# Attention stage of a hybrid retention / sparse-attention block: the spread of the transposed row maxima over four heads moved from VectorE to ScalarE

## The chip, the cores and the metric

The kernel runs on one core of one Trainium2 chip. The metric is the device time of one execution in microseconds (us). Every time below is from such executions, or from one profiled execution of the kernel before.

## The reference

One decoder block over 512 tokens of width 1024: RMSNorm and modulation, one joint input projection, retention (4 heads) beside sparse attention (8 query heads in 2 groups, with compressed, selected and window branches), one output projection, a SwiGLU feed-forward layer (width 2816) and a last RMSNorm. The change lies in the softmax of the selected and the window branch:

```python
s_sel = jnp.einsum('bghqd,bgqnld->bghqnl', qi, k_sel).astype(jnp.float32) * scale
...
p_sel = jax.nn.softmax(s_sel, axis=-1)
o_sel = jnp.einsum('bghqnl,bgqnle->bghqe', p_sel, v_sel)
...
s_win = jnp.einsum('bghqd,bgkd->bghqk', qi, k_win).astype(jnp.float32) * scale
p_win = jax.nn.softmax(jnp.where(m_win, s_win, NEG), axis=-1)
```

A sequence of 512 tokens has 8 blocks of 64, and 16 may be selected, so every causal block is selected. Both branches are therefore plain causal softmaxes over 512 keys, with keys and values of their own.

## The kernel before

The program is written by hand for five in-order engines: TensorE (PE), VectorE (DVE), ScalarE (ACT), GpSimd (POOL) and SyncE (SP). Each has its own function, and they meet only at semaphores. Weights are split into a rounded high part and a low rest, so that each product is three matmuls (`product`). The stages are the input projection (units v = 0 to 23, with attention work mixed into the last ones), an attention loop of slots n = 0 to 41, the output projection, the feed-forward layer and the end.

The attention loop works on eight *blocks* x: x = 2i + b is query tile i (128 queries) in branch b (selected, window). Block x has i + 1 *steps*, one for each key tile; `STEP0` gives the first step of each block. Step s has its scores on PE in slot 2s and its `values` product in slot 2s + 3. Scores are computed transposed (keys on partitions, 4 heads x 128 queries on columns), with their sign turned, so the row maximum to be taken off is a minimum here. It must lie along the columns, the same on all partitions. It is made like this:

- PE `pair(x, h)` (line 1317) computes the scores of head h in the other orientation into banks 4 and 5. DVE `row_min` (line 916) takes the minimum over keys into a column of `mcol`. Head h of group g has column 64g + h.
- PE `max_transpose(x)` (line 1323) turns `mcol` into bank 4 (`ps[:, 4, 0:P]`): row 64g + h now holds the minima of head h. It increments `mx_T`.
- `max_rows(x)` (line 920, on DVE) spreads this over four heads: `MB[:, x % 2, h, :]` is the transposed tile times a column of constants that is -1 in the rows with index h modulo 64 and 0 elsewhere (`K_SEL`). It is one operation, 128x128 in PSUM read four times, 128x512 out. It increments `mb_ok`.
- PE line 1350, the last product of `scores`, multiplies `MB` by a tile of ones and so adds the row to the scores. It waits for `mb_ok`. ACT `exp` (line 610) then takes the exponential out of PSUM into `PT`, and PE `values` (line 1368) multiplies by V.

Banks 4 and 5 are shared. Before PE writes a new group of pairs, another transpose or the scores of retention (line 1411) there, it calls `maxima_free` (line 1301), which waits for everything issued so far: the minima (`mx_min`), the spreads (`mb_ok`) and the retention decays (`r_dec`).

Where each piece stands is fixed by tables of slots:

```python
PAIR_AT = {1: [(4, 0)], 3: [(4, 1)], 6: [(4, 2)], ...
MAX_AT = {0: 2, 2: 3, 9: 4, 17: 5, 23: 6, 31: 7}
SQ_AT = {3: 0, 13: 1, 22: 2, 35: 3}
OUT_AT = {16: 0, 18: 1, 27: 2, 34: 3}
```

`MAX_AT` says that block 2's transpose and spread stand in slot 0, block 3's in slot 2, and so on. Blocks 0 and 1 have theirs in units 21 and 22 of the projection. On PE a slot has its scores first (even slots) or its values (odd slots), then the transpose, and, in the odd slots, the pairs last. On ACT a slot has `exp` first (even slots), then the compressed branch (`cmp_exp`, `cmp_copy`), the squares of retention (`ret_squares`, line 620), the copy of the mix (`mix_high`) and the high part of a weight unit (`high`, line 477). `exp` of step 1 also waits for `r_y`, the retention products of PE line 1425.

Of the kernel before, what the change touches and what calls it, by code (L numbers as in the profile page):

```python
# [9 lines left out]
ALU = mybir.AluOpType  # L10
ACT = mybir.ActivationFunctionType
AX = mybir.AxisListType

P = 128
# [3 lines left out]
NH, NG, HPG, DH = 8, 2, 4, 64  # L18
# [36 lines left out]
MAX_AT = {0: 2, 2: 3, 9: 4, 17: 5, 23: 6, 31: 7}  # L55
# [24 lines left out]
K_SEL = 1030  # L80
# [27 lines left out]
def block_kernel(nc, x, c, ln_mix_g, ln_ffn_g, w_ada, b_ada, w_in, cmp_pe_k, cmp_w1_k, cmp_w2_k,  # L108
# [17 lines left out]
    with ExitStack() as ctx:  # L126
# [25 lines left out]
        cst = at("cst", [P, K_N], F32, 112)  # L152
# [24 lines left out]
        MB = at("MB", [P, 2, HPG, P], F32R, R + 62)  # L177
# [59 lines left out]
        ps = ctx.enter_context(nc.psum_tensor("ps", [P, 8, 512], F32))  # L237
# [31 lines left out]
        mx_ps, mx_min, mx_T, mb_ok, st_ps, p_exp, pv, o_read = (sem(n) for n in ("mx_ps", "mx_min", "mx_T", "mb_ok", "st_ps", "p_exp", "pv", "o_read"))  # L269
# [186 lines left out]
        def _(a):  # L456
# [52 lines left out]
            for k in range(KT):  # L509
                a.wait_ge(mod_read, k // 2 + 1)  # L510
                a.wait_ge(xT_ok, k + 1)
                if k >= 2:
                    a.wait_ge(h_lo, k - 1)
                a.activation(hf[:, k % 2, :], xT[:, k, :], ACT.Identity, bias=mods[:, 1, k:k + 1],
                             scale=mods[:, 0, k:k + 1]).then_inc(h_full, 1)
# [79 lines left out]
            def cmp_exp(i):  # L595
                a.wait_ge(c_pre, i + 1)
                a.activation(pc[:, :, :], sc[:, :, :], ACT.Exp, scale=-1.0).then_inc(c_exp, 1)

            def cmp_copy(i):
                a.wait_ge(c_T, i + 1)  # L600
                a.activation(pcT[:, :, :], ps[:, 6, 0:2 * P].rearrange("p (g q) -> p g q", g=NG), ACT.Copy).then_inc(cT_ok, 1)

            def exp(n):
                for g in range(NG):
                    a.wait_ge(st_ps, NG * n + g + 1)
                    if n == 1:
                        a.wait_ge(r_y, 2)
                    if n >= 2:
                        a.wait_ge(pv, n - 1)
                    a.activation(PT[:, n % 2, g, :], ps[:, g, :], ACT.Exp, scale=-1.0).then_inc(p_exp, 1)  # L610

            def mix_high(i):
                a.wait_ge(mixT_ps, i + 1)
                a.activation(hTh[:, :, i * P:(i + 1) * P], ps[:, 6:8, :].rearrange("p b (k q) -> p (b k) q", k=4),
                             ACT.Copy).then_inc(mix_hi, 1)
# [8 lines left out]
            for v in range(U_IN):  # L624
                for ch in {7: [K_CMP], 8: [K_WIN], 12: [K_Q], 16: [K_RQK], 20: [K_RG]}.get(v, []):
                    evacuate(ch)
                if 2 * UPC <= v + 3 < U_IN:
                    high(v + 3)
                if 9 <= v <= 12:
                    pairs_copy(v - 9)  # L630
                for n in {11: [0, 1], 14: [2, 3], 15: [4, 5], 18: [6, 7], 19: [8, 9]}.get(v, []):
                    rot_high(n)
                if v == 15:
                    a.wait_ge(mlp1, 1)
                    hid = ps[:, 7, 0:2 * NG * CB].rearrange("p (i g n) -> p i g n", i=2, g=NG)
                    a.activation(pbias[:, :], hid[:, :, 0, CB - 1], ACT.Copy).then_inc(mlp1_bias, 1)
                    a.wait_ge(mlp1_bias, 1)
                    for kv in range(2):
                        ins = a.activation(hs[:, kv, :].rearrange("p (g n) -> p g n", g=NG), hid[:, kv, :, 0:CP], ACT.Silu,
                                           bias=pbias[:, kv:kv + 1])  # L640
                    ins.then_inc(mlp1_silu, 1)
                if v == 20:
                    key_high()
                if v == 21:
                    cmp_exp(0)
                if v == 22:
                    cmp_copy(0)
                if v == 23:
                    cmp_exp(1)
# [3 lines left out]
            for n in range(SLOTS):  # L653
                if n % 2 == 0 and n // 2 < STEPS:
                    exp(n // 2)
                if n - 1 in CS_AT:
                    cmp_exp(CS_AT[n - 1])
                if n in CT_AT:
                    cmp_copy(CT_AT[n])
                if n in SQ_AT:  # L660
                    ret_squares(SQ_AT[n])
                if n in M_AT:
                    mix_high(M_AT[n])
                if n in OUT_AT:
                    high(U0_OUT + OUT_AT[n])
# [71 lines left out]
        def _(v_):  # L737
            d = v_
# [178 lines left out]
                                                 accum_out=mcol[:, x % 2, g * DH + h:g * DH + h + 1])  # L917
                ins.then_inc(mx_min, 1)

            def max_rows(x):  # L920

                d.wait_ge(mx_T, x + 1)
                d.tensor_tensor(MB[:, x % 2], ps[:, 4, 0:P].unsqueeze(1).broadcast_to([P, HPG, P]),
                                cst[:, K_SEL:K_SEL + HPG].unsqueeze(2).broadcast_to([P, HPG, P]), ALU.mult).then_inc(mb_ok, 1)

            def heads_view(ap, n=NH):
                return ap.rearrange("p (h x) -> p h x", h=n)

# [88 lines left out]
            for v in range(U_IN):  # L1017
                for n in {11: [0, 1], 14: [2, 3], 15: [4, 5]}.get(v, []):
                    rot_low(n)
                if v == 6:  # L1020
                    for kv in range(2):
                        src = cols[:, 56 + 16 * kv:72 + 16 * kv].unsqueeze(1).broadcast_to([P, NG, CL // 2])
                        ins = d.tensor_copy(pairsT[:, kv, :, T // 2:PAIRS], src)
                    ins.then_inc(pe_cols, 1)
                if v == 11:
                    mod_rows(5, ga1, 0)
                if v == 12:
                    mod_rows(6, ga1, 1)
                if v == 17:
                    mod_columns(7, 2, 32, 0, KT, 48, 16).then_inc(mod_read, 1)  # L1030
                if v == 19:
                    mod_columns(8, 3, 40, 0, KT, 40, None).then_inc(mod_read, 1)
                if v == 20:
                    for t in range(TT):
                        gate_out(t)
                if 2 * UPC <= v < UPC * (K_RQK + 1) + 2 and v % UPC < 2:
                    rope_chunk(v // UPC - 2, (0, 1) if v % UPC == 0 else (2, 3))
                if v == 9:
                    d.wait_ge(proj_ev, TT * (K_WIN + 1))
                    d.tensor_scalar(gates[:, :, :], gates[:, :, :], 0.5, 0.5, ALU.mult, ALU.add).then_inc(gates_ok, 1)  # L1040
                if v == 18:
                    compressed()
                if v == 20:
                    key_low()
                    d.wait_ge(masks_in, 16)
                    d.wait_ge(mcol_set, 1)
                    for h in range(HPG):
                        row_min(0, h)
                if v == 21:
                    max_rows(0)  # L1050
                    cmp_scores(0)
                    for h in range(HPG):
                        row_min(1, h)
                if v == 22:
                    max_rows(1)
                    cmp_gates(0)
                    row_min(2, 0)
                    row_min(2, 1)
                if v == 23:
                    row_min(2, 2)  # L1060
                    row_min(2, 3)
                    cmp_out(0)
                    cmp_scores(1)
                    ret_decay(0, 0)
                    ret_decay(0, 1)
                if 2 * UPC <= v + 3 < U_IN:
                    low(v + 3)
                for j in ada_after.get(v + 3, []):
                    ada(j)
# [6 lines left out]
            for n in range(SLOTS):  # L1076
                if n % 2 and n // 2 in STEP0[1:]:
                    add_branch(STEP0.index(n // 2) - 1)
                for x, h in PAIR_AT.get(n, []):
                    row_min(x, h)  # L1080
                if n in MAX_AT:
                    max_rows(MAX_AT[n])
                if n % 2 and n // 2 in STEP0[1:]:
                    mix_branch(STEP0.index(n // 2) - 1)
                if n in CS_AT:
                    cmp_scores(CS_AT[n])
                if n - 1 in CS_AT:
                    cmp_gates(CS_AT[n - 1])
                if n in CO_AT:
                    cmp_out(CO_AT[n])  # L1090
                if n in RS_AT:
                    ret_decay(*RS_AT[n])
                if n in SQ_AT:
                    ret_var(SQ_AT[n])
                if n in NORM_AT:
                    ret_norm(NORM_AT[n])
                if n in M_AT:
                    mix_low(M_AT[n])
                if n - 1 in OUT_AT:
                    low(U0_OUT + OUT_AT[n - 1])  # L1100
                if n + 1 in OUT_AT:
                    scale_unit(U0_OUT + OUT_AT[n + 1])
# [634 lines left out]
```

## Time and profile before

| | |
|---|---|
| median of 3 runs (lowest, highest) | 698.05 us (697.51, 699.13) |
| the profiled execution: its own time | 698.45 us |
| its span, first to last instruction | 696.6 us |
| PE busy | 671.5 us, 96% |
| DVE busy | 334.2 us, 48% |
| ACT busy | 227.6 us, 33% |
| POOL busy | 187.8 us, 27% |
| mean granted TensorE clock | 0.992 |

A busy share is an average over the whole span. A row of the timeline gives start and length in us, the engine, the line, the operation and its tiles (out<-in), the shape and a count of merged instructions. In brackets stands the idle time of the engine before it, with what ended it. An instruction of an engine can begin a little before the one ahead of it has ended, so that four instructions can take less than four times the length of one.

### The profile page before, as it was taken

The numbers are of one execution on the slowest core, as the hardware profiler recorded it, in microseconds if no ns is written. First come the engines' busy times: TensorE is split into PE (matmuls) and PEld (weight loads), VectorE is DVE, ScalarE is ACT, GpSimd is POOL, SyncE is SP. The second block draws the span as 40 slices with busy tenths as digits, with TensorE's granted clock in tenths as the row PEclk, the third lists the DMA queues.
The fourth block names the chain that finished last, engine by engine and source line by source line (L and its number), as shares of the span: only waits on it lengthen the run. The fifth ranks groups of instructions, "written<-read, shape, count | busy, mean of one in ns | idle before, by whom it ended". The sixth has DMA issues, their size and how long they took to land.

```text
span 696.6 us, 8985 instructions
## 1 busy us (share of the span) xinstructions
PE 671.5 (96%) x3571; PEld 560.8 (80%) x3571; DVE 334.2 (48%) x574; ACT 227.6 (33%) x384; POOL 187.8 (27%) x95
## 2 busy tenths in 40 slices
PE   2799999999999999999999999999999999999996
PEld 1699889887787878888988888888888888888885
DVE  4888988756577874626312531101000039533126
ACT  4546333250243434236432222222222122332224
POOL 2000000000000001050254445534444338455521
PEclk9899999999999999999999999999999999999998
DMA  9988967530000000870054545433432213231003
GB/s 309 362 277 309 384 226 278 208 121 32 0 2 1 1 1 30 248 206 1 3 158 143 152 144 157 121 91 90 121 118 95 91 60 121 95 111 68 0 1 121
DMA packets 74537, 88.08 MB, mean 126 GB/s; under 512 B 3112, under 2 KB 57600, under 8 KB 74368
## 3 DMA queue, kind: packets, MB, share of 16 engines
q1 hardware_dynamic: 73184, 85.31, 37.7%
q10 hardware_dynamic: 896, 1.12, 0.4%
q0 software_dynamic: 416, 1.08, 0.4%
q8 instruction: 28, 0.46, 0.3%
q14 instruction: 13, 0.11, 0.0%
HBM read 85.41 MB, written 2.10 MB: 126 GB/s over the span
## 4 chain that ended last, share of the span: by engine, by line
PE 93%; DVE 3%; issue 1%; DMA 1%; ACT 1%; SPq 0%; POOL 0%; POOLq 0%; DVEq 0%; ACTq 0%
PE ps L1232 14%; PE ps L1233 14%; PE ps L1234 14%; PE ps L1631 12%; PE ps L1632 12%; PE ps L1630 11%; PE ps L1368 5%; PE ps L1425 1%; PE ps L1317 1%; PE ps L1503 1%; DMA xs<-in_x 1%; PE ps L1343 1%; PE ps L1411 1%; PE ps L1245 1%; DVE acc L767 1%
## 5 line engine op out<-in xcount | busy, mean ns | idle before, releaser
L428 POOL TENSOR_TENSOR wl<-raw,wh 128x1024 fp32r<-128x1024 f32 x66 | 172.3, 2615 | 203.4 <-ACT wh L477 203.3
L1630 PE MATMUL ps<-hTh,wh 128*128 128x512 f32 (+1 forms) x384 | 143.6, 374 | 0.0
L1632 PE MATMUL ps<-hTh,wl 128*128 128x512 f32 (+1 forms) x384 | 142.6, 371 | 0.0
L1631 PE MATMUL ps<-hTl,wh 128*128 128x512 f32 (+1 forms) x384 | 142.6, 371 | 0.0
L477 ACT ACTIVATE wh<-raw 128x1024 fp32r<-128x1024 f32 x94 | 97.0, 1038 | 133.9 <-PE ps L1632 74.0
L1162 DVE TENSOR_TENSOR act<-ps,sg 128x512 f32<-128x512 f32 x22 | 15.2, 692 | 195.1 <-PE ps L1632 195.1
L1232 PE MATMUL ps<-wh,hTh 128*128 128x512 f32 (+2 forms) x232 | 90.2, 389 | 2.5 <-DVE hTl L821 2.5
L1233 PE MATMUL ps<-wl,hTh 128*128 128x512 f32 (+2 forms) x232 | 87.3, 376 | 0.0
L1234 PE MATMUL ps<-wh,hTl 128*128 128x512 f32 (+2 forms) x232 | 87.3, 376 | 0.0
L1630 PEld LDWEIGHTS ps<-hTh,wh 128*128 128x128 f32 x384 | 72.4, 188 | 13.0 <-issue 0.5
L1631 PEld LDWEIGHTS ps<-hTl,wh 128*128 128x128 f32 x384 | 72.4, 188 | 12.9 <-issue 0.5
L1632 PEld LDWEIGHTS ps<-hTh,wl 128*128 128x128 f32 x384 | 72.4, 188 | 12.3
L1232 PE MATMUL ps<-wh,ah 128*128 128x512 f32 x176 | 68.5, 389 | 0.0
L1233 PE MATMUL ps<-wl,ah 128*128 128x512 f32 x176 | 68.5, 389 | 0.0
L1234 PE MATMUL ps<-wh,al 128*128 128x512 f32 x176 | 68.5, 389 | 0.0
L1232 PEld LDWEIGHTS ps<-wh,hTh 128*128 128x128 f32 x232 | 44.4, 191 | 11.1 <-issue 3.1
L1157 DVE TENSOR_TENSOR al<-act,ah 128x512 fp32r<-128x512 f32 x22 | 28.3, 1288 | 50.5 <-ACT ah L701 50.5
L1234 PEld LDWEIGHTS ps<-wh,hTl 128*128 128x128 f32 x232 | 44.2, 191 | 8.0
L1233 PEld LDWEIGHTS ps<-wl,hTh 128*128 128x128 f32 x232 | 44.3, 191 | 7.3 <-issue 0.5
L849 DVE TENSOR_TENSOR raw<-raw,ga 128x1024 f32<-128x1024 f32 x30 | 44.8, 1511 | 0.0
L708 ACT ACTIVATE sg<-ps 128x512 f32<-128x512 f32 x22 | 13.2, 598 | 89.4 <-PE ps L1632 89.4
L433 POOL TENSOR_TENSOR yss<-yss,expo 128x4 f32<-128x4 f32 x4 | 5.0, 1242 | 135.9 <-DVE yss L990 135.9
(194 smaller groups left out, 867.4 us busy)
## 6 DMA issues: line engine op xcount, KB each, us to landing
raw<-in_w_ada SPq DMA_DIRECT2D x32, 512.0 KB, 5.4
raw<-in_w_ff_gate SPq DMA_DIRECT2D x22, 512.0 KB, 4.0
raw<-in_w_ff_up SPq DMA_DIRECT2D x22, 512.0 KB, 3.8
raw<-in_w_ff_down SPq DMA_DIRECT2D x22, 512.0 KB, 3.3
raw<-in_w_in SPq DMA_DIRECT2D x20, 512.0 KB, 7.6
early<-in_w_ada SPq DMA_DIRECT2D x16, 512.0 KB, 10.0
raw<-in_w_out SPq DMA_DIRECT2D x8, 512.0 KB, 3.7
xs<-in_x SPq DMA_DIRECT2D x4, 512.0 KB, 5.7
```

Of the source, the lines that this page charges most:

```text
L428: pool.tensor_tensor(lo, raw[:, slot, 0:n], hi.bitcast(F32), ALU.subtract).then_inc(w_lo2, 1)
L477: a.activation(split(u, n)[0], raw[:, slot, 0:n], ACT.Copy).then_inc(w_hi, 1)
L849: d.tensor_tensor(raw[:, slot, :], raw[:, slot, :], ga[:, :], ALU.mult).then_inc(w_scaled, 1)
L1157: d.tensor_tensor(al[:, f % SPLIT, :], act[:, f, :], ah[:, f % SPLIT, :].bitcast(F32), ALU.subtract).then_inc(a_lo, 1)
L1162: d.tensor_tensor(act[:, f, :], ps[:, 2 * (f % 2) + 1, :], sg[:, f % 2, :], ALU.mult).then_inc(act_ok, 1)
L1232: mm(o, ah_, bh_, start=first, stop=False)
L1233: mm(o, ah_, bl_, start=False, stop=False)
L1234: return mm(o, al_, bh_, start=False, stop=last)
L1368: ins = mm(ps[:, 2 + g, h * DE:(h + 1) * DE], PT[:, n % 2, g, h * P:(h + 1) * P], V[:, j, b, g, :], start=j == 0 and h == 0, stop=j == i a ...
L1630: mm(o, hi[:, ks], hTh[:, k, c0:c1], start=k == 0, stop=False)
L1631: mm(o, hi[:, ks], hTl[:, k, c0:c1], start=False, stop=False)
L1632: ins = mm(o, lo[:, ks], hTh[:, k, c0:c1], start=False, stop=k == KT - 1)
```

## The change

`max_rows` leaves DVE and becomes a function of ACT. In place of one multiplication of 128x512 it issues four copies of 128x128, each from bank 4 to one head's part of `MB`, with the column of constants as the copy's scale. Only the last of the four increments `mb_ok`. In units 21 and 22 it stands ahead of `cmp_exp(0)` and `cmp_copy(0)`, in the slots right after `exp`. The program of PE is the same.

```diff
 (in block.scalar)
+            def max_rows(x):
+                a.wait_ge(mx_T, x + 1)
+                for h in range(HPG):
+                    ins = a.activation(MB[:, x % 2, h, :], ps[:, 4, 0:P], ACT.Copy, scale=cst[:, K_SEL + h:K_SEL + h + 1])
+                ins.then_inc(mb_ok, 1)
+
...
                 if v == 21:
+                    max_rows(0)
                     cmp_exp(0)
                 if v == 22:
+                    max_rows(1)
                     cmp_copy(0)
...
             for n in range(SLOTS):
                 if n % 2 == 0 and n // 2 < STEPS:
                     exp(n // 2)
+                if n in MAX_AT:
+                    max_rows(MAX_AT[n])
                 if n - 1 in CS_AT:
...
 (in block.vector)
-            def max_rows(x):
-
-                d.wait_ge(mx_T, x + 1)
-                d.tensor_tensor(MB[:, x % 2], ps[:, 4, 0:P].unsqueeze(1).broadcast_to([P, HPG, P]),
-                                cst[:, K_SEL:K_SEL + HPG].unsqueeze(2).broadcast_to([P, HPG, P]), ALU.mult).then_inc(mb_ok, 1)
...
                 if v == 21:
-                    max_rows(0)
                     cmp_scores(0)
...
                 if v == 22:
-                    max_rows(1)
                     cmp_gates(0)
...
                 for x, h in PAIR_AT.get(n, []):
                     row_min(x, h)
-                if n in MAX_AT:
-                    max_rows(MAX_AT[n])
```

Lines from 612 on are numbered 6 higher in ACT's part of the changed kernel; the copies have line 615, and `ret_squares` goes from 620 to 626.

ACT's program at the start of the attention loop, slots 0 to 4, before (PT<-ps is `exp`, sqj is `ret_squares`, x2 is two instructions alike):

```order
L601 ACTIVATE pcT<-ps 128x256 [waits c_T]
L610 ACTIVATE PT<-ps 128x512 [waits st_ps] x2
L610 ACTIVATE PT<-ps 128x512 [waits r_y,st_ps] x2
L620 ACTIVATE sqj,yss<-ps 128x128 [waits r_y]
L620 ACTIVATE sqj,yss<-ps 128x128 x3
```

and in the changed kernel:

```order
L601 ACTIVATE pcT<-ps 128x256 [waits c_T]
L610 ACTIVATE PT<-ps 128x512 [waits st_ps] x2
L615 ACTIVATE MB<-ps,cst 128x128 [waits mx_T]
L615 ACTIVATE MB<-ps,cst 128x128 x3
L610 ACTIVATE PT<-ps 128x512 [waits r_y,st_ps] x2
L615 ACTIVATE MB<-ps,cst 128x128 [waits mx_T]
L615 ACTIVATE MB<-ps,cst 128x128 x3
L626 ACTIVATE sqj,yss<-ps 128x128 [waits r_y]
L626 ACTIVATE sqj,yss<-ps 128x128 x3
```

The spread of block 2 now stands behind both exponentials of step 0, and that of block 3 behind both of step 1, which wait for `r_y`.

PE's program over the same slots, the same in both kernels (L1323 is the transpose of block 2, then of block 3):

```order
L1323 MATMUL ps<-cst,mcol 128x128 [waits r_dec,mb_ok,mx_min]
L1400 MATMUL ps<-BD,pcT 128x256 [waits c_mix,cT_ok]
L1400 MATMUL ps<-BD,pcT 128x256
L1317 MATMUL ps<-KTh,QTh 128x384 [waits r_dec,mb_ok,mx_min]
L1317 MATMUL ps<-KTh,QTh 128x384
L1343 MATMUL ps<-QTh,KTh 128x512 [waits p_exp]
...
L1323 MATMUL ps<-cst,mcol 128x128 [waits r_dec,mb_ok,mx_min]
L1425 MATMUL ps<-rv,PT 128x128 [waits c_mix,proj_ev,r_dec]
...
L1317 MATMUL ps<-KTh,QTh 128x384 [waits r_dec,mb_ok,mx_min]
```

Nothing moved here. The pair that follows each transpose waits for `mb_ok`, which now comes from ACT.

## Rows read from the trace of the kernel before

**Rows 1.** Busy time in two stretches: us, each engine busy (instructions), clock, DMA, GB/s

```profile
186.00:276.00 90.00, 88.87 (x715) 73.00 (x714) 66.17 (x148) 33.32 (x82) 4.97 (x4) 1.00 0.00 1
320.00:697.00 377.00, 370.46 (x1732) 309.91 (x1731) 112.26 (x131) 108.07 (x151) 166.08 (x68) 0.99 0.31 95
```

**Rows 2.** The chain that ended last, by engine

```profile
PE 93%; DVE 3%; issue 1%; DMA 1%; ACT 1%; SPq 0%; POOL 0%; POOLq 0%; DVEq 0%; ACTq 0%
```

**Rows 3.** Instructions that write MB: ns min/median/max; and whom PE waited for

```profile
L923 DVE TENSOR_TENSOR MB<-ps,cst x8: 680/692/693, 158.6 to 263.3; 128x512 fp32r<-128x512 f32 x8
...
  DVE MB L923: 0.6, 2
```

**Rows 4.** Groups of ACT by shape: busy us, mean ns, idle before

```profile
L683 ACT ACTIVATE h<-ps,mods 128x128 f32<-128x128 f32 x16 | 6.0, 451 | 2.7 <-PE ps L1609 2.7
L620 ACT ACTIVATE sqj<-ps 128x128 f32<-128x128 f32 x16 | 4.2, 285 | 2.7 <-PE ps L1425 2.7
L592 ACT ACTIVATE KCh<-ps,cst 128x32 fp32r<-128x32 f32 x2 | 0.5, 283 | 0.0
```

**Rows 5.** Timeline of ACT: runs of two and of four instructions

```profile
154.65 0.46 ACT L592 ACTIVATE KCh<-ps,cst 128x32 fp32r<-128x32 f32 x2
...
315.67 1.49 ACT L683 ACTIVATE h<-ps,mods 128x128 f32<-128x128 f32 x4
```

**Rows 6.** Timeline, block 0: the spread, and the pairs that wait for it

```profile
158.55 0.68 DVE L923 TENSOR_TENSOR MB<-ps,cst 128x512 fp32r<-128x512 f32 x1
...
159.69 0.66 PE L1317 MATMUL ps<-KTh,QTh 64*128 64x128 f32 x8
```

**Rows 7.** Timeline, blocks 1 and 4: the transpose, and the next pair

```profile
165.31 0.33 PE L1323 MATMUL ps<-cst,mcol 128*128 128x128 f32 x1 [0.67 <-DVE mcol L916]
...
168.32 0.50 PE L1317 MATMUL ps<-KTh,QTh 64*128 64x256 f32 x4
...
204.84 0.28 PE L1323 MATMUL ps<-cst,mcol 128*128 128x128 f32 x1
...
207.89 0.34 PE L1317 MATMUL ps<-KTh,QTh 64*128 64x384 f32 x2
```

**Rows 8.** Timeline, block 2: both exponentials of step 0, the spread, the pair

```profile
186.91 1.09 ACT L610 ACTIVATE PT<-ps 128x512 f32<-128x512 f32 x2 [1.15 <-PE ps L1355]
...
187.25 0.69 DVE L923 TENSOR_TENSOR MB<-ps,cst 128x512 fp32r<-128x512 f32 x1 [0.50 <-PE ps L1323]
188.04 0.44 PE L1317 MATMUL ps<-KTh,QTh 64*128 64x384 f32 x2
```

**Rows 9.** Timeline, block 3: exponentials of step 1, what follows, the pair

```profile
191.24 1.08 ACT L610 ACTIVATE PT<-ps 128x512 f32<-128x512 f32 x2 [3.25 <-PE ps L1425]
192.21 0.28 ACT L620 ACTIVATE sqj<-ps 128x128 f32<-128x128 f32 x1
...
192.80 0.44 PE L1317 MATMUL ps<-KTh,QTh 64*128 64x384 f32 x2
```

**Rows 10.** Timeline, block 5: the spread, and the score matmul that waits

```profile
225.74 0.69 DVE L923 TENSOR_TENSOR MB<-ps,cst 128x512 fp32r<-128x512 f32 x1 [0.56 <-PE ps L1323]
...
226.49 0.51 PE L1350 MATMUL ps<-MB,onesR 64*128 64x512 f32 x2
```

**Rows 11.** Timeline, block 6: the same two

```profile
242.73 0.69 DVE L923 TENSOR_TENSOR MB<-ps,cst 128x512 fp32r<-128x512 f32 x1 [0.43 <-PE ps L1323]
...
243.64 0.40 PE L1350 MATMUL ps<-MB,onesR 64*128 64x512 f32 x2
```

**Rows 12.** Who waited for whom, 186 to 276 us: us, times, longest

```profile
DVE ps L916 <- PE ps L1317: 4.5, 6, 1.8
...
PEld ps L1317 <- DVE mcol L916: 1.3, 3, 0.7
...
PEld ps L1411 <- DVE mcol L916: 0.7, 1, 0.7
...
PE ps L1411 <- DVE hTf L984: 0.5, 1, 0.5
```

## Prediction, made before the changed kernel was run

> **What bounds the kernel now.** I read four views in this order. First the busy time by stretch: from 186 to 276 us, where the attention loop runs, PE is busy 88.87 of 90 us at a granted clock of 1.00, with DVE at 66.17 and ACT at 33.32 [rows 1]. So in this stage as in the others PE sets the pace, and DVE has more work than ACT. Second the chain that ended last: PE holds 93% of it, DVE 3% and ACT 1% [rows 2]. What DVE does is therefore worth only what PE waits for. Third the tile MB: its eight writes take 0.69 us each, and PE waited for them twice, 0.6 us in all [rows 3]. Fourth the timeline around each of the eight spreads, with one question: when is `mb_ok` there, and when does the next PE instruction want it. PE works in order and is nearly always busy, so each 0.1 us by which `mb_ok` comes later than PE wants it is 0.1 us on the end, unless a later wait takes it back.
>
> **What is removed.** Eight VectorE operations of 0.69 us, 5.5 us of DVE time [rows 3]. I cost this at nothing. The cover is PE: DVE is idle in front of most of these operations, because it waits for the transpose (0.50 us before block 2's, 0.56 before block 5's, 0.43 before block 6's [rows 8, 10, 11]), so what stands behind them mostly starts at a later PE event anyway. The exception would be a DVE operation that PE waits for and that stands behind a spread with no idle time between; I come back to it as a rival.
>
> **What is added: the length d of four copies.** The trace has no 128x128 copy out of PSUM with a column as its scale, so I bound it.
> - Nearest from above: four 128x128 operations out of PSUM with two column operands (scale and bias) take 1.49 us together, 0.451 us for one [rows 4, 5]. The step from one to the next is (1.49 - 0.45)/3 = 0.35 us.
> - Without a column operand the same shape takes 0.285 us [rows 4]. One column is therefore worth (0.451 - 0.285)/2 = 0.083 us.
> - So a copy with one column takes 0.37 us and steps by about 0.35 - 0.08 = 0.26 us. Four of them: d = 3 x 0.26 + 0.37 = 1.15 us. I take this, since it differs from the upper row in one operand only.
> - From below: two copies of 128x32 with one column take 0.46 us, 0.283 for one [rows 4, 5], a step of 0.18. Four: 0.82 us, for a quarter of the columns.
>
> So d = 1.15 us, between 0.82 and 1.49, against 0.69 us on DVE. The Trainium skill, on the page "ScalarE: Activation LUTs", section "What ACT_TABLE_LOAD costs", gives 186 ns + 0.833 ns per column, some 93 ns more for each pointer operand, and an overlap of some 93 ns between operations back to back. By it four copies would take an estimated 4 x 386 - 3 x 93 = 1265 ns, and the sum below would be 3.6 us in place of 3.0. No row of this trace has this form, so nothing here says which is right.
>
> **Where the length meets PE.** ACT's successor may start 0.11 us before a pair of exponentials has ended (191.24 + 1.08 = 192.32, and the squares begin at 192.21 [rows 9]), and PE starts 0.06 us after `mb_ok` (225.74 + 0.69 = 226.43, PE at 226.49 [rows 10]). With these two:
>
> 1. Block 2. ACT has the exponentials of step 0 until 186.91 + 1.09 = 188.00 [rows 8], while DVE began the spread at 187.25. So the copies start at 187.89, 0.64 us later than the operation that they replace, and end at 187.89 + d. The next pair, at 188.04 before, can start at 187.95 + d = 189.10. Slip d - 0.09 = **1.06 us**. Everything on PE behind it moves by this.
> 2. Block 3. The exponentials of step 1 wait for the retention products of PE line 1425 [rows 9] and so move by the same 1.06. The copies stand behind them, where the squares stood: they start at 192.21 (+1.06), and the pair can start at 192.27 + d instead of 192.80 (both +1.06). New slip d - 0.53 = **0.62 us**. Here the spread had been long done before; it is the place in ACT's order that makes it late. The squares behind it come 1.15 us later as well, but their reader on DVE stands behind the row minima of the pair that has slipped too.
> 3. Block 5. ACT is free when the transpose ends. The copies start with the old operation, at 225.74, and PE line 1350, which already waited (226.49), starts at 225.80 + d. Slip d - 0.69 = **0.46 us** [rows 10].
> 4. Block 7 has the same pattern, the second of the two waits of [rows 3]: **0.46 us**.
> 5. Block 6. 242.73 + 0.06 + d = 243.94 against 243.64: 0.30 us. PE did not wait here before, and its two matmuls took 0.40 us where the waiting ones of block 5 took 0.51 [rows 10, 11]; with that 0.11 it is **0.41 us**.
> 6. Block 0: if ACT starts no earlier than DVE did, 158.55 + 1.15 + 0.06 = 159.76 against 159.69 [rows 6]. Since ACT is idle there and DVE was not, I count nothing. With d at 1.49 it would be 0.41.
> 7. Blocks 1 and 4: from the start of the transpose to the next pair there are 3.01 and 3.05 us [rows 7]. The transpose (0.33) and d fit twice over. Nothing.
>
> The sum is 1.06 + 0.62 + 0.46 + 0.46 + 0.41 = 3.01 us, and in general 5d - 2.74. For d = 0.82 it is 0.73 + 0.29 + 0.13 + 0.13 + 0 = 1.28; for d = 1.49, with block 0, it is 1.40 + 0.96 + 0.80 + 0.80 + 0.75 + 0.41 = 5.12.
>
> The loads of weights do not cushion it. In the loop DMA moves next to nothing, and from 320 us on PE is busy 370.46 of 377 us [rows 1], so a late start of that stage is a late end. Against the profiled execution's own 698.45 us the sum gives 701.46. The median of the runs shown is 0.40 lower, and to that I apply it: 698.05 + 3.01 = **701.1 us**.
>
> **The rivals.**
>
> *Relief of VectorE: faster.* In the loop PE's two queues waited 1.3 + 0.7 us for row minima and 0.5 us for a decay, 2.5 us together [rows 12]. If DVE's freed time shortened all of them, and the copies were at the cheap end, it would be 1.28 - 2.5 = -1.2 us, 696.8 us. It decides from the point where the slips, 5d - 2.74, are less than what DVE gives back: with the whole 2.5 us below d = 1.05. Against it: in the same stretch DVE's row minima themselves waited 4.5 us for PE's pairs, six times [rows 12]. The minima that PE waits for start when a pair ends, not when DVE comes free.
>
> *The slips are taken back.* If the DVE operations behind those waits do not move when PE moves, the slips of blocks 2 and 3 run into waits that were there already. At most 2.5 of 3.01 us goes: 698.6 us. The same row speaks against it, since those operations are released by PE and move with it.
>
> *The copies cost what the two-operand form costs.* Then it is 698.05 + 5.12 = 703.2 us. For it: the only four-fold 128x128 row of the trace. Against it: one operand less.
>
> **How the numbers follow.** I give the forecast 0.68, with d between 0.95 and 1.3, which is 2.0 to 3.8 us or 700.1 to 701.8. The dear copies get 0.12, the slips taken back 0.12, and relief 0.08. The range reaches down to just under 698.6, and up to 702.9, short of the dear end. That leaves out relief and something over half of the dear case, some 0.15 to 0.2. A measurement of this kernel can tell about 0.2%, 1.4 us, from no change. Slower by more than that, above 699.45, is nearly all of the forecast and the dear case: 0.79. Within it are the slips taken back, half of relief and the forecast's lowest edge: 0.17. Faster is the other half of relief: 0.04.
>
> **What would show it.** In the profile of the changed kernel:
> - eight groups of four copies into MB, each 1.1 to 1.2 us from first start to last end;
> - block 2's copies starting at the end of step 0's exponentials, and the pair behind its transpose about 1 us later than 188.04 with an idle time that ACT's MB ends;
> - waits of PE for MB at blocks 2, 3, 5, 6 and 7, where there were two;
> - PE's output projection starting about 3 us later, and the feed-forward stage as long as before;
> - DVE with 5.5 us less work and as much more idle time.
>
> The prediction is wrong if the copies take under 0.9 us, if the pair after block 2's transpose hardly moves, or if the shift that stands at 195 us is gone by 276.

## The result, and the profile after

| | before | changed |
|---|---|---|
| median of 6 runs | 697.63 us (697.43 to 699.13) | 701.16 us (700.08 to 701.57) |
| ratio, with its 95% interval | | 1.0044 (1.0034 to 1.0054) |
| span of the profiled execution | 696.6 us | 699.6 us |
| DVE busy | 334.2 us | 329.1 us |
| ACT busy | 227.6 us | 236.2 us |
| start of block 0's transpose on PE | 158.10 us | 158.06 us |
| last group of transposes ahead of the feed-forward stage (line 1609) | 332.99 us | 335.96 us |
| from the one to the other | 174.89 us | 177.90 us |

The change costs 3.5 us in the medians, with an interval of 2.4 to 3.8. The last line of the table is the sharper measure, because up to block 0's transpose both programs do the same: 3.01 us. Its end in the kernel before, and the last matmul of the program:

```profile
332.99 1.09 PE L1609 MATMUL ps<-cst,xb 128*128 128x128 f32 x8
...
690.08 0.39 PE L1234 MATMUL ps<-wh,al 128*128 128x512 f32 x1
```

and in the changed kernel:

```profile
335.96 1.09 PE L1609 MATMUL ps<-cst,xb 128*128 128x128 f32 x8
...
693.04 0.39 PE L1234 MATMUL ps<-wh,al 128*128 128x512 f32 x1
```

From block 0's transpose to the last matmul the difference is 3.00 us, so the feed-forward stage is as long as before.

The busy time in three stretches of the changed kernel, as in [rows 1] (us, then PE, PEld, DVE, ACT and POOL busy, clock, DMA share, GB/s):

```profile
186.00:276.00 90.00, 86.44 (x694) 70.75 (x691) 60.50 (x140) 39.22 (x105) 3.33 (x4) 1.00 0.01 1
...
186.00:279.00 93.00, 89.44 (x715) 73.14 (x712) 62.57 (x142) 39.81 (x106) 4.97 (x4) 1.00 0.01 1
...
276.00:320.00 44.00, 44.00 (x228) 37.06 (x228) 19.13 (x25) 14.34 (x21) 12.24 (x7) 1.00 0.63 191
```

PE was 88.87 us busy in the first stretch and now is 86.44, with 21 instructions fewer in it, so PE waits more. The stretch of 93 us has as many matmuls as the 90 us had before (715), and PE is idle for 3.56 us in it, where it was idle for 1.13. The clock is 1.00 in all three. In these 93 us DVE has 142 instructions where it had 148, the six spreads of blocks 2 to 7 being gone, and is busy 3.6 us less (62.57 against 66.17), and nobody gains by it. The 60.50 us up to 276 are lower still because some of DVE's work has slipped past 276.

The tile MB in the changed kernel, as in [rows 3]:

```profile
L615 ACT ACTIVATE MB<-ps,cst x32: 359/370/397, 158.4 to 266.5; 128x128 fp32r<-128x128 f32 x32
...
  PEld ps L1350: 2.1, 3
  PE ps L1350: 0.7, 2
```

One copy takes 0.37 us. PE line 1350 now waits for MB in three places, where there were two short waits. The four copies and their readers, block by block, in the timeline of the changed kernel; first blocks 0 and 1:

```profile
158.37 1.14 ACT L615 ACTIVATE MB<-ps,cst 128x128 fp32r<-128x128 f32 x4 [3.29 <-PE ps L1323]
...
159.53 1.28 ACT L597 ACT_TABLE_LOAD   x1
159.66 0.66 PE L1317 MATMUL ps<-KTh,QTh 64*128 64x128 f32 x8
...
165.64 1.14 ACT L615 ACTIVATE MB<-ps,cst 128x128 fp32r<-128x128 f32 x4 [1.97 <-PE ps L1323]
```

Four copies take 1.14 us. Block 0's end at 159.51, and PE's pair starts at 159.66, as long after the transpose (1.60 us) as before (1.59). Blocks 2 and 3:

```profile
186.89 1.08 ACT L610 ACTIVATE PT<-ps 128x512 f32<-128x512 f32 x2 [1.16 <-PE ps L1355]
...
187.86 1.15 ACT L615 ACTIVATE MB<-ps,cst 128x128 fp32r<-128x128 f32 x4
...
189.11 0.45 PE L1317 MATMUL ps<-KTh,QTh 64*128 64x384 f32 x2 [1.04 <-issue]
...
192.25 1.08 ACT L610 ACTIVATE PT<-ps 128x512 f32<-128x512 f32 x2 [3.24 <-PE ps L1425]
193.22 1.14 ACT L615 ACTIVATE MB<-ps,cst 128x128 fp32r<-128x128 f32 x4
...
194.21 0.31 ACT L626 ACTIVATE sqj<-ps 128x128 f32<-128x128 f32 x1
...
194.46 0.44 PE L1317 MATMUL ps<-KTh,QTh 64*128 64x384 f32 x2 [0.58 <-issue]
```

Both times the copies follow the exponentials, and the pair starts 0.10 us after the last copy has ended. Its row says "issue", which stands where the profile shows nothing that the instruction waited for, and not "ACT MB": the pair waits for up to three semaphores, and the profile found no releaser. That the copies are the releaser is read from the times here and shown by the experiments below. Blocks 5, 6 and 7:

```profile
227.38 1.15 ACT L615 ACTIVATE MB<-ps,cst 128x128 fp32r<-128x128 f32 x4 [1.25 <-PE ps L1323]
228.58 0.51 PE L1350 MATMUL ps<-MB,onesR 64*128 64x512 f32 x2 [0.34 <-ACT MB L615]
...
244.83 1.14 ACT L615 ACTIVATE MB<-ps,cst 128x128 fp32r<-128x128 f32 x4 [0.71 <-PE ps L1323]
...
246.02 0.50 PE L1350 MATMUL ps<-MB,onesR 64*128 64x512 f32 x2
...
265.76 1.14 ACT L615 ACTIVATE MB<-ps,cst 128x128 fp32r<-128x128 f32 x4 [1.21 <-PE ps L1323]
266.95 0.50 PE L1350 MATMUL ps<-MB,onesR 64*128 64x512 f32 x2 [0.34 <-ACT MB L615]
```

Where ACT is free, line 1350 starts 0.05 us after the copies' end. In block 6 it took 0.40 us before and takes 0.50 now.

PE issues the same 3571 matmuls in both kernels, so each can be laid beside its twin. The shift between twins changes at these places and, behind block 0, nowhere else by more than 0.06 us. The largest of the small steps is 0.05 us, taken back at PE line 1425 between blocks 2 and 3.

| block | PE row whose start slips | forecast, us | measured, us |
|---|---|---|---|
| 2 | pair, line 1317 | 1.06 | 1.08 |
| 3 | pair, line 1317 | 0.62 | 0.65 |
| 5 | line 1350 | 0.46 | 0.46 |
| 6 | line 1350, and the row behind it | 0.30 + 0.11 | 0.28 + 0.10 |
| 7 | line 1350 | 0.46 | 0.44 |

### The profile page after: what moved, and what is told of

It is laid out like the page before. It is cut to its first block, busy times and chain, and to the rows that moved or that the text cites. A ratio compares the mean times of both kernels' runs of the same rounds, so it can differ in the third digit from the quotient of the medians.

```text
span 699.6 us, 9009 instructions
## 1 busy us (share of the span) xinstructions
PE 673.1 (96%) x3571; PEld 561.7 (80%) x3571; DVE 329.1 (47%) x566; ACT 236.2 (34%) x416; POOL 187.7 (27%) x95
## 3 DMA queue, kind: packets, MB, share of 16 engines
q0 software_dynamic: 416, 1.08, 0.4%
## 4 chain that ended last, share of the span: by engine, by line
PE 92%; DVE 3%; issue 2%; ACT 1%; DMA 1%; SPq 0%; POOL 0%; POOLq 0%; DVEq 0%; ACTq 0%
PE ps L1232 14%; PE ps L1233 14%; PE ps L1234 13%; PE ps L1631 11%; PE ps L1630 11%; PE ps L1632 11%; PE ps L1368 5%; PE ps L1425 1%; PE ps L1317 1%; PE ps L1503 1%; DMA xs<-in_x 1%; PE ps L1411 1%; PE ps L1245 1%; DVE acc L777 1%; PE ps L1343 1%
```

## The experiments

Each experiment is measured like the last line of the first table: from the start of block 0's transpose to the start of the last group of line 1609, in the profiled execution. I call that the stretch. It leaves out the loading stage at the front, whose end moves from run to run (see the end). Ratios to the kernel before stand beside it where there were several runs.

### One block's engine, or one place in the order

**Blocks 2 and 3 back on VectorE.**

```diff
+ON_DVE = [2, 3]
...
             def max_rows(x):
+                if x in ON_DVE:
+                    return
                 a.wait_ge(mx_T, x + 1)
```

with the old function on VectorE for these two, in its old places.

> The changed kernel with the spread of blocks 2 and 3 back on VectorE; the other six stay four ScalarE copies. My theory (each block's slip is the time by which mb_ok comes later than PE wants it): the slips of blocks 2 and 3, 1.08 and 0.65 us, are gone, those of blocks 5, 6 and 7 stay, 1.3 us in all over the kernel before. Rival, relief: if VectorE's freed time had been buying something, giving two operations back costs part of it, and less than 1.7 us comes back. Rival, the length alone counts and not the place in ScalarE's order: two blocks of five are undone, and only 2 x 0.46 = 0.9 us comes back.

The stretch is 333.01 - 156.78 = 176.23 us, 1.34 over the kernel before; the ratio is 1.0020 (1.0010 to 1.0029). The two pairs have no slip against their twins, and the other three keep 0.45, 0.38 and 0.45. The two blocks account for 1.67 us, as their slips said (1.08 + 0.65, less the 0.05 at line 1425), and giving VectorE its work back cost nothing. Length alone, 0.9 us for two blocks, is out.

**Only blocks 0, 1 and 4 on ScalarE** (`ON_DVE = [2, 3, 5, 6, 7]`).

> Only the spreads of blocks 0, 1 and 4 on ScalarE, the other five on VectorE. My theory: none of these three is wanted by PE before it is there, so the time is that of the kernel before, within 0.1 us in the profile, though VectorE does 2.1 us less. Relief theory: 2.1 us less of VectorE shows as something below the kernel before, up to some tenths of a us.

The stretch is 332.34 - 157.34 = 175.00 us, 0.11 over; the ratio is 1.0001 (0.9991 to 1.0010). Three of the eight spreads move for nothing, in both senses.

**Block 3's copies ahead of the exponentials.**

```diff
             for n in range(SLOTS):
+                if n in (2,):
+                    max_rows(MAX_AT[n])
                 if n % 2 == 0 and n // 2 < STEPS:
                     exp(n // 2)
-                if n in MAX_AT:
+                if n in MAX_AT and n not in (2,):
                     max_rows(MAX_AT[n])
```

> The changed kernel with ScalarE's order swapped in one slot: the copies of block 3 stand ahead of the exponentials of step 1, not behind them. My theory: those exponentials wait for PE's retention products anyway, the copies fit in front of them (they end some 0.1 us after the exponentials used to start), and block 3's slip of 0.65 us is gone: 2.4 us over the kernel before. Rival, length: the copies take as long as before, so the slip stays.

In the timeline of this kernel:

```profile
191.02 1.14 ACT L615 ACTIVATE MB<-ps,cst 128x128 fp32r<-128x128 f32 x4 [2.28 <-PE ps L1325]
...
192.03 1.10 ACT L610 ACTIVATE PT<-ps 128x512 f32<-128x512 f32 x2
```

The copies use time in which ScalarE stood idle, and the exponentials follow at once. The stretch is 335.05 - 157.80 = 177.25 us, 2.36 over the kernel before and 0.65 under the changed one. For block 3 the whole cost was the place in the order. The runs could not have told this: their ratio is 1.0044 (1.0027 to 1.0061), that of the changed kernel.

**Blocks 2 and 3 both ahead** (slots 0 and 2).

> The changed kernel with the copies of blocks 2 and 3 both ahead of the exponentials of their step. My theory for block 2: the copies end some 0.65 us earlier and the pair behind the transpose slips by 0.4 in place of 1.08 us, but the exponentials of step 0 now end at about 189.4 and PE line 1343 waits for them, so PE is late by the same 1.1 us one instruction further on; block 3 has no slip. In all as with block 3 alone put ahead, 2.4 us over the kernel before, or 0.1 more. Rival, the exponentials have room: 0.7 us comes back at block 2 as well, 1.7 over the kernel before.

The stretch is 334.72 - 157.32 = 177.40 us, 2.51 over, in one profile. In the timeline of this kernel, at block 2:

```profile
186.50 1.14 ACT L615 ACTIVATE MB<-ps,cst 128x128 fp32r<-128x128 f32 x4 [1.51 <-PE ps L1325]
...
187.51 1.10 ACT L610 ACTIVATE PT<-ps 128x512 f32<-128x512 f32 x2
187.74 0.44 PE L1319 MATMUL ps<-KTh,QTh 64*128 64x384 f32 x2 [0.41 <-issue]
...
188.66 0.50 PE L1345 MATMUL ps<-QTh,KTh 64*128 64x512 f32 x2 [0.49 <-ACT PT L610]
```

The pair slips by 0.44 us only, but the next score matmuls (line 1343 of the kernel before, 1345 here) wait for the exponentials, which start 1.35 us later than they would have (187.51, where the exponentials used to begin 0.03 us before the transpose, here at 186.19). They add 0.68 us, and the row behind them 0.14. So block 2 costs 1.26 us instead of 1.08. Neither order is free for block 2: PE wants the copies and the exponentials of step 0 at nearly the same time. In the kernel before, line 1343 started right behind the pair at 188.04:

```profile
188.29 0.42 PE L1343 MATMUL ps<-QTh,KTh 64*128 64x512 f32 x2
```

The copies between the two exponentials were not tried. An estimate from these rows: from 186.91 on, both exponentials and four copies take 1.09 + 1.14 - 0.11 = 2.12 us back to back, to 189.03, while PE wants the last of them by 188.3. So that order could not be free either, but it might cost some 0.8 us in place of 1.08.

### Is VectorE's freed time worth anything?

**VectorE filled again.** In the eight places where it did the spread, VectorE waits for the same transpose and does an operation of the same length into a tile that nobody reads:

```diff
+            def fill(x):
+                d.wait_ge(mx_T, x + 1)
+                d.tensor_tensor(spare[:, :], masks[:, :], masks[:, :], ALU.mult)
```

> The changed kernel, and in the eight places where VectorE did the spread it now waits for the same transpose and does one 128x512 operation of the same length on SBUF into a tile that nobody reads. So VectorE has its old load back. My theory: the freed time was worth nothing, and the time is that of the changed kernel within 0.1 us in the profile. Relief theory: the change was dearer than 3.0 us and VectorE's relief hid part of it; then this kernel is slower than the changed one by up to 2.5 us.

The group of these operations by shape (busy us, mean ns):

```profile
L934 DVE TENSOR_TENSOR spare<-masks 128x512 f32<-128x512 f32 x8 | 5.5, 692 | 3.1 <-PE ps L1333 3.1
```

It is the old load to 0.1 us. The stretch is 335.45 - 157.57 = 177.88 us, against 177.90 for the changed kernel: no difference. Nor did PE's waits for VectorE shrink when the time was free. The waits of the changed kernel from 186 to 276 us, to be held against [rows 12]:

```profile
DVE ps L926 <- PE ps L1317: 5.3, 7, 1.9
...
PEld ps L1317 <- DVE mcol L926: 1.3, 3, 0.7
...
PEld ps L1411 <- DVE mcol L926: 0.8, 1, 0.8
...
PE ps L1411 <- DVE hTf L988: 0.5, 1, 0.5
```

They are 2.6 us in place of 2.5. These minima start when a pair of PE ends, and a free VectorE starts them no sooner.

### Is it the length of the copies?

**A fifth copy of the same form**, ahead of the four:

```diff
                 a.wait_ge(mx_T, x + 1)
+                a.activation(spare[:, :], ps[:, 4, 0:P], ACT.Copy, scale=cst[:, K_SEL:K_SEL + 1])
                 for h in range(HPG):
```

> The changed kernel with a fifth copy of the same form ahead of the four, into a tile that nobody reads. The four took d = 1.14 us with a step of 0.26. My theory: the end moves by one step for each block whose spread PE waits for (2, 3, 5, 6 and 7), 5 x 0.25 = 1.3 us, and block 0, which had 0.09 us to spare, loses 0.17: from the first transpose to the last matmul 1.5 us more than the changed kernel, 4.5 more than before. Rival, the cost is a fixed wait for ScalarE (its place in the order, the semaphore) and not the length: about the changed kernel's time.

**The same with a plain number as its scale** (`scale=-1.0`).

> As the kernel with five copies, but the fifth has a plain number as its scale in place of a column. My theory: a column operand costs some 0.09 us of the step, so this copy adds 0.17 us per block and not 0.25: 0.9 us over the changed kernel, 3.9 over the kernel before. Rival, the price sits in the number of instructions, whatever their operand: the same as the kernel with five.

The stretches are 336.43 - 156.98 = 179.45 and 336.63 - 157.78 = 178.85 us, that is 4.56 and 3.96 over the kernel before, each in one profile. Block by block the fifth copy adds 0.26 us to the slips of blocks 2, 3, 5, 6 and 7, and block 0, which had no slip, gets 0.26 as well, where 0.17 was expected: it had next to no time to spare. The plain copy adds 0.16 to 0.18 in the five, and 0.17 in block 0. The two forms on ScalarE, first with the column, then with the number:

```profile
157.28 0.37 ACT L615 ACTIVATE spare<-ps,cst 128x128 fp32r<-128x128 f32 x1 [3.30 <-PE ps L1325]
157.55 1.14 ACT L617 ACTIVATE MB<-ps,cst 128x128 fp32r<-128x128 f32 x4
```

```profile
158.08 0.28 ACT L615 ACTIVATE spare<-ps 128x128 fp32r<-128x128 f32 x1 [3.30 <-PE ps L1325]
158.26 1.13 ACT L617 ACTIVATE MB<-ps,cst 128x128 fp32r<-128x128 f32 x4
```

A column costs 0.09 us, in the length (0.37 against 0.28) as in the step (0.27 against 0.18). So at each of these blocks the length of the run passes to the end one to one.

### A wait of the kernel before that can go

The timeline showed another delay, which has nothing to do with the change: PE's transpose of block 1 waited for its minima ([rows 7], 0.67 us idle), while VectorE had stood idle for the compressed branch's scores. In the kernel before, the first operation on these scores and the exponential of the compressed branch:

```profile
161.84 0.49 DVE L953 TENSOR_TENSOR sc<-ps,cst 128x128 f32<-128x128 f32 x2 [2.61 <-PE ps L1234]
...
163.28 0.42 ACT L597 ACTIVATE pc<-sc 128x256 f32<-128x256 f32 x1 [6.87 <-DVE sc L958]
```

```diff
                 if v == 21:
                     max_rows(0)
-                    cmp_scores(0)
                     for h in range(HPG):
                         row_min(1, h)
+                    cmp_scores(0)
```

> Not the change, but the kernel before with VectorE's order swapped in unit 21: the row minima of block 1 ahead of the compressed branch's scores. Before, VectorE stood idle for 2.6 us waiting for those scores, with block 1's pairs done, and PE's transpose of block 1 then waited for the minima, a gap of 0.8 us at 165.3. Expected: that gap closes, 0.7 us less from the first transpose to the last matmul. Rival: the compressed branch gets later by the length of the minima and PE's transposes of it wait; then no gain.

The stretch is 331.29 - 157.29 = 174.00 us, 0.89 us less than before, where 0.7 was expected. Against the twins 0.82 us go at this transpose and 0.06 at the matmul behind it; no other step is over 0.03. In the timeline of this kernel:

```profile
161.54 0.49 DVE L953 TENSOR_TENSOR sc<-ps,cst 128x128 f32<-128x128 f32 x2
...
162.97 0.42 ACT L597 ACTIVATE pc<-sc 128x256 f32<-128x256 f32 x1 [7.38 <-DVE sc L958]
163.45 0.14 PEld L1323 LDWEIGHTS ps<-cst,mcol 128*128 128x128 f32 x1
163.67 0.27 PE L1323 MATMUL ps<-cst,mcol 128*128 128x128 f32 x1
...
167.05 0.44 PE L1388 MATMUL ps<-cst,pc 128*128 128x128 f32 x2
```

The compressed branch does get later: its exponential starts 5.68 us after block 0's transpose (162.97 - 157.29), where it was 5.18. But it ends at 163.39, and PE reads its result only at 167.05, so nobody waits for these 0.5 us.

Over 11 runs of it and 15 of the kernel before the ratio is 0.9990 (0.9981 to 0.9999), 697.29 against 697.82 us: faster than both kernels, by an amount that the runs just tell from nothing.

**Both harmless edits together**: this order, and only blocks 0, 1 and 4 on ScalarE.

> The two harmless edits together: the spreads of blocks 0, 1 and 4 on ScalarE, the other five on VectorE, and the row minima of block 1 ahead of the compressed branch's scores. My theory: as the kernel with that order alone, 0.8 to 0.9 us less than before from the first transpose to the last matmul, since VectorE's 2.1 us less is worth nothing. Rival: with VectorE's order tightened its freed time starts to count, and some tenths of a us more come off.

The stretch is 331.08 - 157.06 = 174.02 us, the same as with the order alone. The ratio is 0.9989 (0.9980 to 0.9998). Even with VectorE's order tightened, its freed time buys nothing that can be seen.

## Why the prediction was right

1. *The bound and the question.* PE sets the pace, so only the arrival of `mb_ok` counts. It held: five slips, each at a place that the prediction named, make up the whole difference of the stretch. Of them only 0.05 us was taken back, at line 1425.
2. *The length d.* 1.15 us was forecast, 1.14 to 1.15 measured. The step was given as 0.26, and is. The row with two operands less one operand was the right anchor; the lower bound was 0.3 us too cheap, the upper 0.35 too dear. The Trainium skill ("ScalarE: Activation LUTs", "What ACT_TABLE_LOAD costs") has the price of a column operand right, 93 ns against 0.09 us here. The estimate by it for a single copy is nearly right as well, 386 ns against 0.37 us. Its overlap of some 93 ns is smaller than the 0.11 us of these rows; with the 16 ns too much on each copy, the estimate by it for four, 1265 ns, is 0.12 us too long, and a sum of 3.6 us would have been 0.6 too high.
3. *The queue.* Blocks 2 and 3, where the copies stand behind the exponentials, were given 1.68 us and took 1.73. One small term was mis-sized: the pair starts 0.10 us after the copies' end, not 0.06. With d at 1.14 for 1.15, that accounts for the 0.05 us more. With both on VectorE 1.67 us came back. The experiments sharpen one thing: in block 3 all of it was ScalarE's order, and in block 2 neither of the two orders tried is free.
4. *The three blocks with ScalarE free*, 5, 6 and 7: 1.33 forecast, 1.28 measured. The extra 0.11 us for line 1350 in block 6 came as 0.10.
5. *Blocks 0, 1 and 4* at nothing. The kernel with only these on ScalarE shows it. By the prediction's own sum block 0 would have been 0.07 us late (159.76 against 159.69), had ScalarE started no earlier than VectorE. It started 0.31 us after the transpose, where VectorE had started after 0.45, and that saved it. There was next to nothing to spare: one more copy put all of its 0.26 us on PE.
6. *VectorE's 5.5 us at nothing.* Shown twice, by filling it again and by leaving it free in three blocks.
7. *The sum.* 3.01 us forecast, 3.01 in the stretch. The medians differ by 3.5 us, of which the profiles give 3.0. The interval, 2.4 to 3.8, holds both, and what the other half of a microsecond is stays open; the front of the kernel alone moves by more than that from profile to profile. That the median, 701.16 us, lies so near the forecast of 701.1 is in part luck: the forecast started from 698.05 us for the kernel before, and the median of its six runs is 697.63.

Two signs were told wrongly. The prediction expected the idle time ahead of the pairs to be ended by "ACT's MB"; the rows say "issue", as they did before the change, and so the profile names MB as a wait in three blocks and not in five. And DVE's busy time fell by 5.1 us, not 5.5, since an operation begins a little before the one ahead of it has ended.

Of the rivals, relief is out, and so are slips that are taken back (against the twins the largest step down behind block 0 is 0.05 us) and the dear copies.

## What to carry to other kernels

Where one engine is busy all the time, ask of a piece of work that is to be moved not how busy its old and new engines are but when its result is wanted, and what stands ahead of it in the new engine's order at that moment. The engine with a third of the load was the wrong place for five of eight spreads: in two the copies stood behind exponentials (in block 2 ScalarE was at work on them, in block 3 it was still waiting to start them), and in three one operation in four pieces was simply longer, 1.14 us against 0.69. The three spreads that nobody waited for could be moved freely, and moving them gained nothing.

A difference of 1 us in 700 is better read from one stretch of two profiles, row beside row, than from the medians of a few runs. Here each kernel has one profile, and three pairs of kernels that should not differ agree within 0.02, 0.02 and 0.11 us in the stretch.

## What I had not expected

The front of the kernel, before anything that these edits touch, ends at different times. Block 0's transpose began between 156.78 and 158.10 us in eleven profiles, with the same PE program up to there:

```profile
156.78 0.27 PE L1337 MATMUL ps<-cst,mcol 128*128 128x128 f32 x1
```

```profile
158.10 0.27 PE L1323 MATMUL ps<-cst,mcol 128*128 128x128 f32 x1
```

The first is the kernel with blocks 2 and 3 on VectorE, the second the kernel before. That is 1.3 us, more than most of the slips here, and it explains why the whole spans (696.6, and 696.7 with a real 1.34 us more) nearly agree. What moves it was not tried.

The table load of ScalarE went from 155.12 us, right behind the keys' copies, to 159.53, behind block 0's spread, because the first exponential now comes after four waiting copies. In all nine profiles with block 0's copies on ScalarE it starts where they end. It still had 2.4 us to spare before that exponential, at 163.25, but a load that used to lie in an idle stretch can end up behind a wait.
